# First mixture of experts: four groups of four experts, one TensorE strip per expert, instead of eight pairs

## What is computed

```python
def hier_moe(h, lp):                     # t: 256 tokens x 1024
    g_logits = t @ moe_rg_w + moe_rg_b   # 4 groups, the best one is taken
    p_top, g_sel = top_k(softmax(g_logits), 1)
    e_logits = (t @ moe_re_w + moe_re_b).reshape(256, 4, 4)
    e_top, e_sel = top_k(e_logits of the group taken, 2)   # two of its four experts
    combine = one_hot(g_sel * 4 + e_sel) * (p_top * softmax(e_top))
    hg, hu = t @ w_gate[e], t @ w_up[e]  # 16 experts, 1024 -> 256 each
    a = silu(hg) * hu * combine[e]
    return sum over e of a @ w_down[e]   # 256 -> 1024
```

## Time and profile before

| | us |
|---|---|
| median of 3 runs | 1922.81 (1921.26 to 1925.93) |
| span of the profiled execution | 1921.8 |
| TensorE busy in it | 1839.2 (96%) |
| VectorE, ScalarE, GpSimd busy | 686.0, 312.4, 26.5 |
| first gate-up to last down projection of the first mixture | 131.2 |
| share of that stretch in the span | 7% |

### The profile page before, as it was taken

How to read it: one execution, slowest core, us unless ns; L and a number is a source line. 1 busy time by engine, 2 the same in 40 slices (tenths; PEclk the granted TensorE clock), 3 DMA queues, 4 the chain that set the end, 5 groups by cost and what they waited for, 6 DMA issues and landing times.

```text
span 1921.8 us, 39001 instructions
## 1 busy us (share of the span) xinstructions
PE 1839.2 (96%) x17396; PEld 1079.3 (56%) x17396; DVE 686.0 (36%) x1668; ACT 312.4 (16%) x729; POOL 26.5 (1%) x41
## 2 busy tenths in 40 slices
PE   6999989999888899999999999999999999999997
PEld 2655767885777555577776555343444444343443
DVE  3757772622433565433323553311011111111023
ACT  3221121001222324200001242100000010000001
POOL 0100000000000000000000000100000000000000
PEclk9999999999999999999999999999999999999999
DMA  9968743254699442477675323799999999999995
GB/s 356 366 228 301 268 156 128 89 178 167 251 396 369 154 162 102 154 246 256 221 258 173 131 104 124 297 399 420 410 419 409 416 411 405 420 413 415 409 416 216
DMA packets 156047, 538.84 MB, mean 280 GB/s; under 512 B 10016, under 2 KB 34944, under 8 KB 121712
## 3 DMA queue, kind: packets, MB, share of 16 engines
q1 hardware_dynamic: 149360, 509.15, 68.8%
q0 software_dynamic: 3728, 17.58, 2.6%
q10 hardware_dynamic: 2784, 9.53, 1.3%
HBM read 527.18 MB, written 12.19 MB: 281 GB/s over the span
## 4 chain that ended last, share of the span: by engine, by line
PE 88%; DVE 6%; DMA 2%; issue 2%; DVEq 1%; ACT 1%; SPq 0%; ACTq 0%
PE ps L1279 24%; PE ps L1315 12%; PE ps L1513 8%; PE ps L1225 8%; PE ps L1089 4%; PE ps L1207 4%; PE ps L1237 4%; PE ps L892 4%; PE ps L1291 3%; PE ps L1104 2%; PE ps L1333 2%; PE ps L1302 1%; PE ps L757 1%; PE ps L699 1%; DMA ring<-in_ada_w 1%
## 5 line engine op out<-in xcount | busy, mean ns | idle before, releaser
L1279 PE MATMUL ps<-ring,arena 128*32 128x512 f32 (+1 forms) x4608 | 459.1, 557 | 0.0
L1279 PEld LDWEIGHTS ps<-ring,arena 128*32 128x32 f32 x4608 | 148.9, 110 | 294.0 <-issue 289.1
L1315 PE MATMUL ps<-ring,arena 128*32 128x256 f32 x4224 | 232.1, 379 | 0.0
L1315 PEld LDWEIGHTS ps<-ring,arena 128*32 128x32 f32 x4224 | 137.3, 110 | 98.7 <-issue 12.0
L2864 DVE TENSOR_TENSOR arena<-arena,ps 128x256 f32<-128x256 f32 (+1 forms) x72 | 26.8, 373 | 391.0 <-ACT arena L1965 391.0
L1513 PE MATMUL ps<-ring,hT 128*128 128x512 f32 (+1 forms) x384 | 155.9, 556 | 1.1 <-DVE hT L2214 1.1
L1225 PE MATMUL ps<-hT,ring 128*128 128x256 f32 x704 | 153.8, 379 | 0.8 <-DVE hT L2214 0.8
L1225 PEld LDWEIGHTS ps<-hT,ring 128*128 128x128 f32 x704 | 133.6, 190 | 23.4 <-issue 5.7
L1513 PEld LDWEIGHTS ps<-ring,hT 128*128 128x128 f32 x384 | 69.5, 191 | 69.2 <-issue 67.3
L2758 DVE TENSOR_SCALAR arena<-ps,ga,mod 128x128 f32<-128x128 f32 (+1 forms) x64 | 20.8, 388 | 200.9 <-PE ps L1330 118.1
L1965 ACT ACTIVATE arena<-ps 128x256 f32<-128x256 f32 (+1 forms) x72 | 21.2, 367 | 422.0 <-PE ps L1279 422.0
(11 more groups left out here) (427 smaller groups left out, 1801.2 us busy)
## 6 DMA issues: line engine op xcount, KB each, us to landing
ring<-in_gate_up SPq DMA_DIRECT2D x160, 1024.0 KB, 14.0
ring<-in_down SPq DMA_DIRECT2D x104, 1024.0 KB, 14.6
ring<-in_gate_up_last SPq DMA_DIRECT2D x64, 768.0 KB, 14.4
ring<-in_w_ada SPq DMA_DIRECT2D x48, 768.0 KB, 6.1
ring<-in_w_in SPq DMA_DIRECT2D x36, 768.0 KB, 7.6
ring<-in_ada_w SPq DMA_DIRECT2D x24, 768.0 KB, 9.3
ring<-in_w_ada SPq DMA_DIRECT2D x24, 512.0 KB, 7.1
ring<-in_w_in SPq DMA_DIRECT2D x12, 1024.0 KB, 7.4
```

Source lines behind the costliest of these rows:

```text
L1279: last = mm(ps[32 * q:32 * q + 32, base + t_, 0:2 * n], src[:, k, 32 * t_:32 * t_ + 32], w[:, q], start=k == 0, stop=k == KD - 1)
L1315: last = mm(ps[32 * q:32 * q + 32, bank + t_ // 2, (t_ % 2) * 256:(t_ % 2 + 1) * 256], rows[:, t_, o:o + 32], cells[:, cell, r * D + q * 2 ...
```

## The change

The 16 experts are worked off in 4 groups of 4, which are the groups of the routing. The unit is now a group and one block of 128 tokens, a piece; each expert has 32 slots per piece, so that a piece has 128 rows: 32 per expert, and the strip e of the array works for expert e.

- The gather takes one token block per piece, so nothing is summed: 8 matmuls a piece in place of 16 a job.
- Gate and up: per slice of 128 inputs and piece four matmuls, one per expert, each on its 32 rows with that expert's 512 columns (gate 256, up 256).
- The product of SiLU and up is turned by TensorE (`turn_act`), ScalarE copies it back (`act_turned`).
- Down: per cell (half of the hidden width, half of the output) and piece four matmuls of 512 columns.
- The rows leave PSUM multiplied by the gate row (`y_in`), and TensorE spreads them to the tokens by the transposed weighted selection (`turn_weights`, `spread`), for every group; VectorE adds the result into `x` (`add_rows`). The stores, GpSimd's part and the weighing are gone.
- The host packs the weights so that a cell has one slice of inputs for four experts, or one quarter of the down matrix for four.
- The limit is now 32 per expert and block; above it the engines run `every` (not shown), where every group takes every token over the full array.
- `gate_half` stands ahead of the count; two fillers at the start are gone.

The core of the diff (TensorE, then ScalarE and VectorE; the rest of the second mixture is renamed only):

```diff
-J1 = E1 // 2
+G1, PER_GROUP = 4, 4
-STAGES = ([("moe1", 6 * J1, 1), ...
+STAGES = ([("moe1", (KD + 4) * G1, 1), ...
-CAP = {"moe1": 64, "moe2": 96}
+CAP = {"moe1": 32, "moe2": 96}
...
+    def gather(n):
+        g, b = divmod(n, NT)
+        pe.wait_ge(sem("moe1_sel"), n + 1)
+        if n >= 2:
+            pe.wait_ge(sem("moe1_he_low"), n)
+            pe.wait_ge(sem("moe1_he_high"), n)
+        for k in range(KD):
+            last = mm(ps[:, piece_bank(n) + k // 4, (k % 4) * P:(k % 4 + 1) * P], xn2[:, b, k * P:(k + 1) * P], g_sel[:, b, :],
+                      start=True, stop=True)
+        last.then_inc(sem("moe1_gathered"), 1)
+    def gate_up(g, k, b):
+        w = cell_of(gu[g][k])
+        for e in range(PER_GROUP):
+            last = mm(ps[32 * e:32 * e + 32, b, :], g_he[:, g % 2, b, k * P + 32 * e:k * P + 32 * e + 32],
+                      w[:, e * 512:(e + 1) * 512], start=k == 0, stop=k == KD - 1)
...
+    def turn_act(g, b):
+        pe.wait_ge(sem("moe1_act"), 2 * g + b + 1)
+        if b:
+            turn_weights(g)
+        for r in range(2):
+            last = nc.tensor.transpose(ps[:, b, r * P:(r + 1) * P], g_act[:, b, r * P:(r + 1) * P], ident)
+        last.then_inc(sem("moe1_act_turned"), 1)
+    def turn_weights(g):
+        pe.wait_ge(sem("moe1_selw"), 2 * g + 2)
+        for b in range(NT):
+            nc.tensor.transpose(ps[:, 1, (2 + b) * P:(3 + b) * P], g_selw[:, g % 2, b * P:(b + 1) * P], ident)
+    def down(g):
+        for c, entry in enumerate(dn[g]):
+            half, r = divmod(c, 2)
+            w = cell_of(entry)
+            for b in range(NT):
+                if c == 0:
+                    pe.wait_ge(sem("moe1_actT"), 2 * g + b + 1)
+                    if g:
+                        pe.wait_ge(sem("moe1_added"), 2 * g - 1 + b)
+                for e in range(PER_GROUP):
+                    last = mm(ps[32 * e:32 * e + 32, 4 + 2 * b + half, :], g_actT[:, b, r, 32 * e:32 * e + 32],
+                              w[:, e * 512:(e + 1) * 512], start=r == 0, stop=r == 1)
+            last.then_inc(used, 1)
+    def spread(g):
+        pe.wait_ge(sem("moe1_selT"), g + 1)
+        for b in range(NT):
+            pe.wait_ge(sem("moe1_y"), 4 * g + 3 + b)
+            for half in range(2):
+                last = mm(ps[:, 4 + 2 * b + half, :], g_selT[:, b, :], g_y[:, b, half * 512:(half + 1) * 512], start=True, stop=True)
+            last.then_inc(sem("moe1_spread"), 1)
+    def common():
+        gather(0)
+        gather(1)
+        for g in range(G1):
+            for b in range(NT):
+                pe.wait_ge(sem("moe1_he_low"), 2 * g + b + 1)
+                pe.wait_ge(sem("moe1_he_high"), 2 * g + b + 1)
...
+                gate_up(g, 0, b)
+                gate_up(g, 1, b)
+            for k in range(2, KD):
+                gate_up(g, k, 0)
+                gate_up(g, k, 1)
+                if k == 3 and g:
+                    spread(g - 1)
+                elif k == 5 and g + 1 < G1:
+                    gather(2 * g + 2)
+            if g + 1 < G1:
+                gather(2 * g + 3)
+            turn_act(g, 0)
+            turn_act(g, 1)
+            down(g)
+        spread(G1 - 1)
+        busy(26, 0)
...
             router("x2", 0)
+            gate_half(1, 0, 4)
+            gate_half(1, 1, 5)
             busy(3, 0)
-            moe_mm("moe1", 0)
+            moe1_mm()
...
+    def y_in(g, half):                       # VectorE
+        dve.wait_ge(used, dn[g][2 * half + 1][3])
+        for b in range(NT):
+            v.tensor_tensor(g_y[:, b, half * 512:(half + 1) * 512], ps[:, 4 + 2 * b + half, :],
+                            grow[:, 1, half * 512:(half + 1) * 512], ALU.mult).then_inc(sem("moe1_y"), 1)
+    def add_rows(g, b):
+        dve.wait_ge(sem("moe1_spread"), 2 * g + b + 1)
+        last = v.tensor_tensor(x[:, b, :], x[:, b, :], all_ps[:, 2048 + b * D:2048 + (b + 1) * D], ALU.add)
```

More of the change, by code:

```diff
@@ L687, in _ @@
+            pool.drain()
         @block.tensor
@@ new lines, in moe2_mm, with gate_up @@
+            def moe2_mm():
+                jobs, (gu, dn) = E2, PLAN["moe2"]
+                final = len(WIDTHS) - 1
+                sel, selT, ye = region(R_SE, NT, SLOT_N), region(R_ST, T)[0:SLOT_N], region(R_YE, D)[0:SLOT_N]
+                he, actT, actT8 = region(R_HE, 2, KD, SLOT_N), region(R_MT, 2, 4, T), region(R_MT, 8, T)
+                count_slots(1, E2, True)
+                busy(2, 2)
+                over = too_many(1)
+                def gate_up(k, entry, n, blocks, src, base, count):
+                    cell = entry[0]
+                    pe.wait_ge(cell_full[cell], count)
+                    w = cells[:, cell, 0:8 * n].rearrange("p (b q c) -> p q b c", q=4, c=32)
+                    for t_ in range(blocks):
+                        for q in range(4):
+                            last = mm(ps[32 * q:32 * q + 32, base + t_, 0:2 * n], src[:, k, 32 * t_:32 * t_ + 32],
+                                      w[:, q], start=k == 0, stop=k == KD - 1)
@@ new lines, in gather @@
+                        dst = ps[:, x0 + k // 4, (k % 4) * SLOT_N:(k % 4 + 1) * SLOT_N]
+                        if j:
+                            last = nc.tensor.transpose(dst, fetch[j % 2][0:SLOT_N, k * P:(k + 1) * P], ident[0:SLOT_N, 0:SLOT_N])
+                        else:
+                            for b in range(NT):
+                                last = mm_strips(dst, xn2[:, b, k * P:(k + 1) * P], sel[:, b, :], start=b == 0, stop=b == NT - 1)
+                    if j == jobs - 1:
+                        for b in range(NT):
+                            last = nc.tensor.transpose(ps[0:SLOT_N, x0 + 2, b * P:(b + 1) * P], sel[:, b, :], ident)
@@ L1385, in small @@
                     gathered = 1
-                    for s in range(len(steps) + 1):
+                    for s in range(len(STEPS) + 1):
                         a0, x0 = 3 * (s % 2), 3 * ((s + 1) % 2)
@@ L2748, in moe_act @@
-                if i == 0:
-                    for half in range(2):
-                        gate_half_in(1, half, 4 + half, 2 + half)
-                dve.wait_ge(sem("flag"), i + 1)
-                over = dve.value_load(flags[P - 1:P, i:i + 1], min_val=0, max_val=1)
+                        last = v.tensor_scalar(sel[:, b, :], iota[:, 0:cap], slots[:, b, j:j + 1], None, ALU.is_equal)
+                    last.then_inc(sem("moe2_sel"), 1)
+                select(0)
+                weights2()
```

763 lines of the change are left out of this document (384 added, 379 removed).

## The result

The kernel after takes 1896.3 us (median of four runs, 1894.32 to 1896.96); the kernel before, measured beside it, 1922.03 us (1920.91 to 1925.93). The ratio is 0.9863, with an interval of 0.9849 to 0.9877: faster by 25.7 us. 1894 was forecast, and 1887 to 1906 as the range. Of the two profiled executions the span falls from 1921.8 to 1894.9 us, by 26.9, and the instructions from 39001 to 34995.

A forecast was written before the change was run, and what follows sets the result against it. TensorE's own order in the first mixture was taken as the bound; -18.3 - 1.9 - 6.1 - 2.0 = -28.3 us from the 1921.8 us span gave 1893.5, as median 1894, with 1887 to 1906 as the 8-in-10 range.

The forecast's parts named there:

- Groups: First mixture, from first gate-up to end of last down projection: 112.9 us instead of 131.2, -18.3 us.
- the waits: In the first mixture: copies, uncovered SiLU and product, second block's input, loose ends; 3.0 us, from 1.5 to 6.
- The reading of the gaps: Gate-up's 12.6 us of idle, following counts of 128 records, are instructions arriving too late; taken as gone.
- Start: Gate rows move ahead of the count; first gate-up at 502.0 us instead of 503.93, -1.9 us.
- the flag "as before": Ahead of the first gathers: flag written at 494.48 + 0.15 as in the kernel before, but no longer covered.
- Tail: Last down projection to the next stage's transposes (L825): 21.9 to 15.8 us, -6.1 us, the filler being late.
- `x`'s chain: Behind the last down projection: x's spread, additions and products need 12.0 us, less than the filler's 15.8.
- Clock and turn: L825 and first L1513 no longer at half clock: 4.03 us there becomes some 3.0, as much saved behind; -2.0 us.
- The weights as the bound: Rival: loading the first mixture's weights sets its pace; 1899 us, at worst 1904; chance 0.12.
- The gaps stay: Rival: gate-up gaps aren't fetching, or fetching still trails; 12.6 us and the clock come back, 1907 us; chance 0.07.
- The serial steps: Rival: act, turn, copy, down cost 2 to 3 us per group with nothing behind on TensorE; 1902 us; chance 0.10.
- The other arm: Rival: a token count above 32 runs every expert over all 256 tokens; over 200 us slower, about 2130; chance 0.02.

The follow-up runs named there:

- the kernel with 2.39: Kernel after with 14 fillers at the end, 4 between count and flag, and the late norm weights' wait moved to first use: 1890.75 us, ratio to before 0.9852.

## Why the prediction was right, and where its steps were off

**Groups: -20.3 us against -18.3.** From start to start on the timeline after, the terms are gate-up 56.5 (55.4 forecast), down 27.7 (27.7), gather 11.6 (12.5, which held some half clock), spread 10.9 (10.7), turning 3.8 (3.6), and the waits 0.4 in place of 3.0. The waits carry the difference. The reading of the gaps was right, and the three kernels with 128-column pieces or half a load show it. But the forecast took their price as 12.6 us; by the halved load it is 17.2 us, with the half clock and the slower records behind them, 85% of what the groups won. Turning, copies and the additions to `x` cost what their cover promised.

**Start: -0.9 us against -1.9.** The step that failed is the flag "as before" and with it the gathers in "3.8 to 7.5 us, as the clock goes": I took 502.0 for the first gate-up, it was 503.35. The flag is written 9.28 us behind the router where it was 8.52, because VectorE's wait for the late norm weights, which lies ahead of it, grew from 0.66 to 1.41 us. With the gate rows gone from behind the count TensorE stands idle through it, 3.00 us in all, and gathers at half clock. The length of that wait is an accident of the traced execution: with the same code it is 0.96 to 1.70 us in five traces, and the start 15.31 to 17.41 us, with the 16.0 of the forecast between them. Without the wait the start is 14.55 us, 3.4 shorter than before. So the sign was right and the size of this miss is partly chance. The branch on VectorE cost under 1.22 us, inside the bounds.

**Tail: -4.4 us against -6.1.** The filler was indeed what is late, and `x`'s chain 12.2 us where 12.0 was forecast. What the sum lacked is the jump over the other arm, 1.69 us behind the filler. The jump stands in the kernel before as well; no idle there is put down to it, and the 3.38 us of wait for `x` would cover it.

**Clock and turn: -2.3 us against -2.0**, 1.3 in the turn and 1.0 in the first projection, in nearly equal halves as forecast. L823 and the projection start at full clock, although the jump stands before them.

**The rivals.** The weights as the bound: out, the groups are the same with half of them. The gaps stay: out for 512 and for 256 columns. The serial steps: 0.42 us in the last group, not 2 to 3 per group. The other arm: not taken, the stage has the strip forms only. So the time came out right because misses cancelled: 2.0 us more than forecast in the groups and 0.3 in the turn, against 1.0 and 1.7 less in start and tail. As far as the time goes, that is luck.

## What to carry to other kernels

Idle time of an engine that nothing in the profile explains is worth counting in instructions: where gaps stand a fixed number of records apart and shrink when the DMA engines have less to move, fewer and longer matmuls win more than the work that they save, here 17 of 20 us. When work is moved out from behind a wait, ask what the engine does in its place, since an idle TensorE can be paid for again at half clock, here with 6.68 us for gathers that take 3.73 at full clock. And a microsecond in one trace's start is not yet the edit's: ask first whether a wait ahead of it has changed. And a filler that covers a wait can hide other late things with it, here a jump of 1.7 us, which is due once the wait is gone.

## What was not expected of the hardware

- TensorE resumes 2.2 to 2.9 us behind the start of the quarter microsecond in which a 16 KB instruction packet is recorded, at a gap in straight code and behind a taken branch alike.
- The jump over the other arm shows as 1.67 to 2.02 us of idle behind 26 fillers (six kernels), as 2.39 and 2.92 behind 14, and as 3.18 and 3.75 where only the spread is ahead of it. The packet comes 1.25 us before the work ahead ends in the kernel after, 0.5 us before it in the kernel with 2.39, and 0.07, 0.35 and 0.86 us after it in the other three; from the packet on it is 2.8 to 2.9 us in all five. The DMA share in the idle time was 0.02 in the kernel after and 1.04 to 1.07 in those four. Whether the load or the shorter cover holds the packet up stays open.
- Idle time alone does not set the clock: behind 3.18 us of it the granted clock was 0.54, behind 3.75 us in another kernel 1.00 (617.13 to 622.80). What decides this no run here tells.
